# A decoder trunk in one core: the first feed-forward group in ordinary form, the squares summed on VectorE

## The reference, cut to what matters

```
def rmsnorm(x, g):
    y = x * lax.rsqrt(jnp.mean(x * x, axis=-1, keepdims=True) + EPS)
    return y * g

def swiglu(x, w_in, w_out):
    gate, up = jnp.split(x @ w_in, 2, axis=-1)
    return (jax.nn.silu(gate) * up) @ w_out

for layer in range(DEPTH):
    mix = recurrent_mixer(...) if layer < N_A else forgetting_attention(...)
    h = h + mix
    h = h + swiglu(rmsnorm(h, norm_ffn[layer]), w_ffn_in[layer], w_ffn_out[layer])
return rmsnorm(h, norm_final)
```

## Time and profile before

| | us |
|---|---|
| median of 3 runs | 2400.66 (2400.25 to 2406.35) |
| the profiled execution | 2403.73 |
| its span, first to last instruction | 2401.9 |
| TensorE busy in it | 2329.1 |
| VectorE busy in it | 1423.8 |
| ScalarE busy in it | 893.8 |
| GpSimd busy in it | 164.9 |

### The profile page before, as it was taken

How to read it: one execution, slowest core, us unless ns; L and a number is a source line. 1 busy time by engine, 2 the same in 40 slices (tenths; PEclk the granted TensorE clock), 3 DMA queues, 4 the chain that set the end, 5 groups by cost and what they waited for, 6 DMA issues and landing times.

```text
span 2401.9 us, 28970 instructions
## 1 busy us (share of the span) xinstructions
PE 2329.1 (97%) x10945; PEld 1922.3 (80%) x10945; DVE 1423.8 (59%) x1589; ACT 893.8 (37%) x1289; POOL 164.9 (7%) x97
## 2 busy tenths in 40 slices
PE   8999968999999999989999999999999999999998
PEld 7788846888888888778888878778888888888886
DVE  7667787666666666676666656753433334344435
ACT  5553644222222222255656656643211111111114
POOL 3000020000000000041111111102000000000000
PEclk9999989999999999999999999999999999999999
DMA  4121101111111111121111011122111111111111
GB/s 141 44 61 52 53 0 50 54 53 54 53 53 52 52 53 53 54 80 32 31 36 35 27 36 36 53 89 70 53 45 51 44 52 44 52 44 52 44 44 70
DMA packets 167310, 123.41 MB, mean 51 GB/s; under 512 B 5081, under 2 KB 148673, under 8 KB 167233
## 3 DMA queue, kind: packets, MB, share of 16 engines
q1 hardware_dynamic: 165504, 118.04, 16.1%
q10 hardware_dynamic: 1728, 4.31, 0.7%
HBM read 113.89 MB, written 8.45 MB: 51 GB/s over the span
## 4 chain that ended last, share of the span: by engine, by line
PE 79%; DVE 2%; issue 1%; ACT 1%; DMA 0%; POOL 0%; ACTq 0%; DVEq 0%; SPq 0%
PE ps L879 39%; PE ps L1051 16%; PE ps L1231 10%; PE ps L1278 3%; PE ps L1265 3%; PE ps L1365 3%; PE ps L1246 2%; PE ps L1243 1%; PE ps L1204 1%; PE ps L1344 1%; PE ps L1245 0%; PE ps L1311 0%; DVE xl L1960 0%; PE ps L1190 0%; DVE resid L1976 0%
## 5 line engine op out<-in xcount | busy, mean ns | idle before, releaser
L1976 DVE TENSOR_TENSOR resid<-ps,resid 128x1024 f32<-128x1024 f32 x204 | 247.9, 1221 | 151.8 <-PE ps L879 151.8
L1970 DVE TENSOR_TENSOR tmp<-ps,rstd 128x1024 f32<-128x1024 f32 x52 | 63.4, 1223 | 268.9 <-PE ps L879 268.4
L879 PE MATMUL ps<-x1h,wh_att 128*128 128x512 f32 x528 | 163.1, 390 | 0.0
L879 PE MATMUL ps<-x1l,wh_att 128*128 128x512 f32 x528 | 162.6, 389 | 0.0
L879 PE MATMUL ps<-x1h,wl_att 128*128 128x512 f32 x528 | 162.6, 389 | 0.0
L2212 DVE TENSOR_TENSOR ring_l<-raw_ffn,ring_h 128x512 fp32r<-128x512 f32 x154 | 108.2, 709 | 90.4 <-ACT ring_h L1588 90.2
L1588 ACT ACTIVATE ring_h<-raw_ffn 128x512 fp32r<-128x512 f32 x154 | 95.2, 626 | 177.1 <-PE ps L879 99.7
L1231 PE MATMUL ps<-xh,wh_att 128*128 128x512 f32 x368 | 150.1, 408 | 1.4 <-issue 1.4
L1231 PE MATMUL ps<-xl,wh_att 128*128 128x512 f32 x368 | 144.8, 393 | 2.4 <-issue 2.4
L1231 PE MATMUL ps<-xh,wl_att 128*128 128x512 f32 x368 | 144.9, 394 | 0.0
L1939 DVE TENSOR_TENSOR wl_att<-raw_att,wh_att 128x1024 fp32r<-128x1024 f32 x75 | 104.2, 1390 | 60.8 <-ACT wh_att L1409 60.8
(11 more groups left out here) (354 smaller groups left out, 5539.7 us busy)
## 6 DMA issues: line engine op xcount, KB each, us to landing
raw_ffn<-in_w_ffn_in SPq DMA_DIRECT2D x44, 512.0 KB, 5.0
raw_att<-in_w_ffn_in SPq DMA_DIRECT2D x33, 512.0 KB, 3.8
raw_ffn<-in_w_ffn_out SPq DMA_DIRECT2D x22, 512.0 KB, 4.3
raw<-in_w_rec_in SPq DMA_DIRECT2D x16, 512.0 KB, 5.6
raw_att<-in_w_kvf SPq DMA_DIRECT2D x16, 512.0 KB, 4.0
raw<-in_w_ffn_in SPq DMA_DIRECT2D x11, 512.0 KB, 3.8
raw<-in_w_ffn_out SPq DMA_DIRECT2D x11, 512.0 KB, 3.5
raw_att<-in_w_ffn_out SPq DMA_DIRECT2D x11, 512.0 KB, 3.5
```

The costliest lines, as they stand in the source:

```text
L879: last = pe.matmul(acc[:, h], w, v[:, h], start=(first and p == 0), stop=(final and p == 2))
L1976: dve.tensor_tensor(resid[:, m, :], ps[slot][:, :], resid[:, m, :], ALU.add).then_inc(drained[slot], 1)
```

## The change

The first group no longer uses seven products on sums, but eight on plain quarters for each pair: 16 products. B12 is made for it, in the buffers of T4 (high) and T3 (low), which it leaves after the thirteenth product. The four weight blocks of pair 0 are each one unit and serve two products (both token halves), those of pair 1 as well. Gate and up of the two pairs stand in four PSUM tiles of their own; there are no taps and joins in this group, and VectorE scales each tile at once (`first_gate`, `first_up`). The sums T1 and T2 are made behind the plain quarters, T3 and T4 behind the norm, between steps of the first group's end. ScalarE scales the difference twice now (into the high half of T1 and into `t2_sum`), where VectorE scaled it once before. The sums of squares of this place go from GpSimd to VectorE (`sum_square`). The stat stands behind the tenth product. The first load of group 1 waits for four units instead of thirteen. In group 1, pair 0 waits for two scaled tiles, and its P5 unit is made before the group. Functions take an object F with the block's semaphores and buffers; what they do is else the same. Of the diff, lines that only rename are left out:

```diff
+class FeedForward:
+    def __init__(self, f, seg, order, first_units):
+        self.f, self.seg, self.order = f, seg, order
+        self.first_units = first_units + ["g1", "g2", "u1", "u2"]
+        self.first_products = [(0, n, half) for half in range(2) for n in range(4)]
+        self.first_products += [(1, n, half) for of in (4, 6) for half in (1, 0) for n in (of, of + 1)]
+    def first_part(self, n, half):
+        return {"1": ("B11", "B12"), "2": ("B21", "B22")}[self.first_units[n][1]][half]
...
     GROUP_UNITS, OUT_UNIT, SECOND_UNIT = 18, 7, 11
-    UNITS_FIRST = len(FIRST_GROUP)
-    PART_HIGHS = [(c, k) for k in range(4) for c in ("B21", "B22")]
...
+    UNITS_FIRST, PRODUCTS_FIRST, B12_USED, STAT_AFTER = 8, 16, 13, 9
+    T_SUMS = [("D", 0), ("D", 1), ("T2", 0), ("D", 2), ("T2", 1), ("D", 3), ("T2", 2), ("T2", 3)]
+    T_SUMS += [(c, k) for c in ("T3", "T4") for k in range(4)]
...
+    PART_HIGHS = [(c, k) for c in ("B21", "B11", "B22", "B12") for k in range(4)] + T_HIGHS
+    PART_LOWS = [(c, k) for c in ("B21", "B11", "B22", "B12") for k in range(4)] + T_LOWS
...
+            part_h["B12"], part_l["B12"] = part_h["T4"], part_l["T3"]
...
-                return (product_filled, off - RING + 1) if off >= RING else (in_filled, 4 * BLOCKS)
+                return (F.product_filled, off + 1) if off >= RING else (in_filled, 4 * BLOCKS)
...
-                sp.wait_ge(unit_lo, UNITS_FIRST - 1 if first else unit(g, SECOND_UNIT - GROUP_UNITS)[1] - 1)
...
+                sp.wait_ge(F.unit_lo, 4 if first else unit(g, SECOND_UNIT - GROUP_UNITS)[1] - 1)
+                load_pair(F, g, 0, load_of(g, 0))
...
             pool.wait_ge(hi_ready[slot], n)
-            run_squares("recE")
             gain_piece(pieces.use("forget", 0), V_KV, HEADS)
...
+            def first_group(F):
+                begun = set()
+                for n, (j, u, half) in enumerate(F.first_products):
+                    up = F.first_units[u][0] == "u"
+                    tile = first_tile(F, j, up)
+                    if tile not in begun:
+                        claim(tile)
+                    start = (tile, half) not in begun
+                    begun.update((tile, (tile, half)))
+                    product(F, bank(tile[0], half), unit(0, u), F.first_part(u, half), start, True, PART_LOWS)
+                    if n == STAT_AFTER:
+                        run_stat(F.seg)
...
+                lows = PART_LOWS if isinstance(g, int) and g == 1 and j == 0 else None
+                if lows is not None:
+                    for t in range(2):
+                        slot, n = first_tile(F, 0, t)
+                        pe.wait_ge(drained[slot], n)
+                else:
...
-            last_y_high(1)
...
+                elif c == "T1":
+                    g = V_FFN + F.f * KT + k
+                    act.wait_ge(F.t_summed, T_SUMS.index(("D", k)) + 1)
+                    act.activation(F.part_h[c][:, k, :], F.t_sum[k % 2][:, :], ACT.Copy,
+                                   scale=vec[:, g:g + 1]).then_inc(F.part_hi, 1)
+                    act.activation(F.t2_sum[:, k, :], F.t_sum[k % 2][:, :], ACT.Copy,
...
+            def rec_to_ffn(F):
+                for n in range(4):
+                    first_high(F, n)
+                last_y_high(1)
                 for k in range(4):
+                    part_high(F, "B21", k)
                     square("recE", k)
+                for c in ("B11", "B22", "B12"):
+                    for k in range(4):
+                        part_high(F, c, k)
+                square("recE", 4)
+                first_high(F, 4)
+                square("recE", 5)
+                part_high(F, "T1", 0)
+                first_high(F, 5)
+                square("recE", 6)
+                part_high(F, "T1", 1)
+                first_high(F, 6)
+                square("recE", 7)
+                part_high(F, "T2", 0)
+                first_high(F, 7)
+                part_high(F, "T1", 2)
+                part_high(F, "T2", 1)
+                part_high(F, "T1", 3)
+                part_high(F, "T2", 2)
+                part_high(F, "T2", 3)
+                root("recE")
+                pair_silu(F, 0, 0)
+                pair_high(F, 1, 0, P1)
+                pair_high(F, 1, 0, P2)
                 for k in range(4):
+                    part_high(F, "T3", k)
+                hidden_high(F, 0, 0)
+                pair_high(F, 1, 0, P6)
+                pair_high(F, 1, 0, P5)
                 for k in range(4):
...
+                pair_silu(F, prev, 1)
+                if not (isinstance(g, int) and g == 1):
+                    pair_high(F, g, 0, P5)
+                tap(F, g, 0, "s1")
...
+                    dve.wait_ge(F.t_scaled, k + 1)
+                    ins = dve.scalar_tensor_tensor(out=t2, in0=r22, scalar=g2, in1=t2, op0=ALU.mult, op1=ALU.subtract)
...
+            def sum_square(seg, k):
+                dve.wait_ge(sq_ready, STAT[seg] * KT + k + 1)
+                if k > 1:
+                    dve.wait_ge(sq_summed, SUMMED[seg] + k - 1)
+                dve.tensor_tensor(sq(seg, 0), sq(seg, 0), sq(seg, k), ALU.add).then_inc(sq_summed, 1)
+            def rec_to_ffn(F):
                 def add(n):
                     add_tile(tiles.use("recE", n), feature("recE", n), 8 * (BLOCKS - 1) + n + 1)
+                first_low(F, 0)
+                first_low(F, 1)
+                add(0)
+                for n in range(1, 5):
+                    add(n)
+                    part_low(F, "B21", n - 1)
+                first_low(F, 2)
+                for n in range(5, 8):
+                    add(n)
+                    part_low(F, "B11", n - 5)
+                part_low(F, "B11", 3)
+                first_low(F, 3)
+                for c in ("B22", "B12"):
+                    for k in range(4):
+                        part_low(F, c, k)
+                for k in range(1, 4):
+                    sum_square("recE", k)
+                part_sum(F, "D", 0)
+                first_low(F, 4)
+                sum_square("recE", 4)
+                part_sum(F, "D", 1)
+                first_low(F, 5)
+                sum_square("recE", 5)
+                part_sum(F, "T2", 0)
+                part_low(F, "T1", 0)
+                first_low(F, 6)
+                sum_square("recE", 6)
+                part_sum(F, "D", 2)
+                part_low(F, "T2", 0)
+                first_low(F, 7)
+                sum_square("recE", 7)
+                part_sum(F, "T2", 1)
+                part_low(F, "T1", 1)
+                part_sum(F, "D", 3)
+                part_low(F, "T2", 1)
+                part_sum(F, "T2", 2)
+                part_low(F, "T1", 2)
+                part_low(F, "T2", 2)
+                part_sum(F, "T2", 3)
+                part_low(F, "T1", 3)
+                part_low(F, "T2", 3)
                 norm_ready("recE")
+                first_gate(F, 0)
+                first_up(F, 0)
+                weight_sum(F, 1, 0, 1, 2)
+                pair_low(F, 1, 0, P1)
+                gate_times_up(F, 0, 0)
+                pair_low(F, 1, 0, P2)
+                late_parts(F, "T3")
+                hidden_low(F, 0, 0)
+                weight_sum(F, 1, 0, 3)
+                pair_low(F, 1, 0, P6)
+                pair_low(F, 1, 0, P5)
+                first_gate(F, 1)
```

More of the change, by code:

```diff
@@ L544, in bank, with first_filled, banks @@
+        def first_filled(F, j, up):
+            last = max(n for n, (_, u, _) in enumerate(F.first_products)
+                       if u // 4 == j and (F.first_units[u][0] == "u") == bool(up))
+            return F.product_filled, last + 1
         def bank(tile, half):
             return ps[tile][:, half * BANK:(half + 1) * BANK]
-        def banks(j, first=False):
-            return bank(0, j), bank(1, 0), bank(1, 0) if first and j == 1 else bank(1, 1)
+        def banks(j):
+            return bank(0, j), bank(1, 0), bank(1, 1)
@@ L551, in ffn_free, with resid_tile @@
+        def resid_tile(F, m):
+            return tiles.use(F.seg, F.order.index(m))
         def ffn_free(f, j, g):
@@ L1640, in first_group, with tap @@
-            def first_group():
-                def high(n):
-                    pair_high(0, *FIRST_GROUP[n])
-                high(0)
-                high(1)
+                unit_high(F, unit(g, off), raw_block(F, b, n), (F.loaded[b], count), unit_freed(F, g, off))
+            def tap(F, g, j, what):
+                w, _, y = banks(j)
+                act.wait_ge(F.product_filled, product_at(g, PRODUCTS * j + {"s1": P1, "u2": P6, "s5": P5}[what]))
+                act.wait_ge(hl_ready if what == "s5" else h_ready, times(g, 2, 2 * F.f * GROUPS + j - 1))
+                gate, up = F.gate_up[j]
+                dst = {"s1": gate[:, 0:BANK], "u2": gate[:, BANK:S], "s5": up[:, BANK:S]}[what]
+                act.activation(dst, y if what == "s5" else w, ACT.Copy).then_inc(F.tapped, 1)
@@ new lines, in groups @@
+            def groups(F):
```

(12 more changed lines are left out.)

722 lines of the change are left out of this document (313 added, 409 removed).

## The result

The changed kernel takes 2378.34 us in the median of four runs (2376.64 to 2380.36), the kernel before 2403.06 in the four runs beside it (2400.25 to 2406.35): a ratio of 0.9897, with a 95% interval from 0.9879 to 0.9915. It is faster by 24.7 us. The profiled execution took 2376.64 us, of which the span is 2374.8, 27.1 us less than the span of the profile before.

A forecast was written before the change was run, and what follows sets the result against it. TensorE, busy 97%, was the bound, with VectorE bounding it from 338 to 364 us. P6 of group 1 at 391.1 with low clock, against 411.31, gave 20.2 us off 2400.66: 2380.5 us, range 2374 to 2388.5.

The forecast's parts named there:

- Residual tiles: Before the first group: tile 4 starts at 319.9 us instead of 323.97, its 4.57 us wait becoming about 0.5.
- The sixteen products: First group on TensorE: two products more, +5.5 us, no waits inside; the stat ends at 359.9, all sixteen at 376.3.
- the ledger: Account up to P6 of group 1: gone 26.0 us of waits and some 9.5 of low clock, added together 15.4.
- Squares on VectorE: Seven sums of squares moved from GpSimd to VectorE: between 1.7 us gained and 8.3 lost, booked at 8.3 in VectorE's chain.
- The rival that blamed ScalarE: VectorE's slow operations come from ScalarE's work and stay, 2.1 us each on the path; up to 2419 us; chance 0.04.
- The chain to the tap: VectorE and ScalarE up to group 1's first tap: root from 361.9 to 366.6 us, T4 until 388.0, tap done 389.5.
- The new wait: P6 of group 1 waits for ScalarE's tap until 389.5 us: 7.8 us instead of 6.03, bounds nothing and 14.
- The clock behind it: Low TensorE clock after P6's wait for the tap, priced at 1.6 us from one row.
- Behind P6: From P6 of group 1 both kernels issue the same instructions; from 430 us all starts earlier and runs as before.
- the second wait: Rival: VectorE falls behind from 340 to 366 us, the root is late, cover 1.1 us; 2385 to 2389 us; chance 0.14.
- The shorter wait: Rival: P6's wait for the tap is shorter, at most 7.8 + 1.6 us; down to 2371 us; chance 0.08.
- the time did not return in group 1: Rival: the waits' time returns elsewhere in group 1, nothing gained; 2394 to 2405 us; chance 0.04.

## Why the prediction came out as it did

I had forecast 2380.5 us (2374.0 to 2388.5); it is 2378.34. The sum for the first group held almost to the step. That the time is off by only 2.2 us is in part luck: the gain was forecast as 20.2 us and is 24.7, because a term of about 5 us behind the group was missing; but the kernel before took 2403.06 us in the runs beside this one and not the 2400.66 from which the forecast was counted, which hides half of the error.

*Residual tiles.* Tile 4 starts at 319.90, forecast 319.9; its wait is 0.39, forecast 0.5. Full clock from 324 to 330 us, as forecast.

*The sixteen products.* No wait in any of them, the stat at 358.12 (forecast 358.2). The choice to call these 5.5 us "on the path, certain" was wrong as a price, though: the run with fewer matmuls shows them free. The forecast did not suffer, because I had P6 wait for the tap and not for TensorE; only the ledger did. The ledger booked 5.5 us of products beside 7.8 of wait, when the two are one sum: 13.3 us between TensorE's work and the tap, however it is divided.

*Squares on VectorE.* Differences at 0.69 us, GpSimd idle. That GpSimd was the cause is shown twice, by taking its sums away (0.69) and by putting them back (2.90). The rival that blamed ScalarE has fallen: with the sums moved, ScalarE's copy (0.72 us) and the difference (0.69) both start at 336.10, and in the kernel before ScalarE's squares end just before the long differences begin (338.42 and 338.58 us). The rule of the Trainium skill, SBUF — State Buffer, "Who interferes with whom", that the two engines block one another agrees with the trace in both directions: VectorE's sum for T2 rose from 0.75 to 2.90 us, and GpSimd's sum, where it was the one held up, from 2.36 to 3.60 us. The advice in the Trainium skill, Perfetto Trace Analysis, "Optimizing Scalar/DVE Operations", to move work off a saturated VectorE would by itself have had the change lose, though the same place warns that it may not help between these two engines; moving seven sums onto it cost nothing that can be measured in the old order (0.9991, 0.9973 to 1.0010) and gave 1.6 us at P6 in the new one. Of the two ends that I had set (1.7 us of gain, 8.3 of loss) it came out at the gain. Most of the forecast hung on the order, and rightly.

*The chain to the tap.* The root's first load at 362.10 (forecast 361.9), its end at 366.79 (366.6), the last high half of T4 at 388.12 (388.0), Silu and tap until 389.55 (389.5). ScalarE's timeline:

```profile
387.49 0.63 ACT L1695 ACTIVATE t4h<-t_sum 128x512 fp32r<-128x512 f32 x1 [0.83 <-DVE t_sum L2383]
388.02 1.04 ACT L1666 ACTIVATE gate<-gate 128x1024 f32<-128x1024 f32 x1
388.97 0.58 ACT L1658 ACTIVATE gate<-ps 128x512 f32<-128x512 f32 x1
```

The new wait is 7.79 us (7.8). Every instruction of the chain was costed from a row, and its order read from the diff; the chain holds to 0.2 us over 70 us. With the clock of 0.72 at the first residual tiles it comes 1.7 us later; that this differs between executions I had not allowed for, and the range covered it.

*The clock behind it.* Priced at 1.6 us from the wait of 6.03, it was 2.1 for this wait of 7.79: this term was mis-sized by 0.5 us, and the group gives 19.6 us instead of 20.2. The length of the wait doesn't explain it. In the kernels in the old order the same twelve matmuls cost 1.5 us of low clock behind 5.83 us of wait, 1.6 behind 6.03, 2.2 behind 5.94, 2.4 behind 5.89 and 2.6 behind 5.62. One row of one profile could not give this price to better than about 1 us.

*Behind P6.* Here a step failed: that from 430 us on "everything behind it starts earlier, and runs as it did". It does so until about 1390 us; then the kernel before loses time to waits that the one after doesn't have. 5.8 us in the two profiles, for one pair of waits of 3.7 us together, and 1.4 near 1605 us; in the medians 24.7 - 19.6 = 5.1 us for all that lies behind P5. The row was there to be seen: two waits without a releaser in a loop whose matmuls have all operands. I had looked for TensorE's idle time only in the stretch of the change. It couldn't have been foreseen that the change would take them away; that the 2403 us held such a part could have been a rival with its price: the 3.7 us of these waits, and the low clock behind them.

The rivals: the second wait did not come (no wait for the stat's bank), though the profile with the sums on GpSimd shows how near it was: 0.6 us. The shorter wait did not come, and the time did not return in group 1.

## What to carry to other kernels

Where one engine's queue orders the work, write out its instructions with a duration from a row for each, and do so up to the instruction that the bottleneck waits for: here the sum held to 0.2 us over 70, and the chain showed where a better order was to be had (the T4 round behind the taps, another 6.9 us). The clock behind a wait is known less well: take several rows for it. Work added to the bottleneck ahead of a wait for another engine costs nothing but makes that wait shorter; book the two as one term. Before two versions of a kernel with loops are compared, look for waits without a releaser in both traces, outside the changed stretch too, and try a few idle instructions ahead of the loop: what they move there is not the merit of either version. Compare marks only between profiles whose clock agrees ahead of them.

## What was not expected of the hardware

TensorE stopped 2 or 4 times in an execution for 1.3 to 2.8 us in the attention loop, with its operands there, in all six profiles with the old number of its matmuls ahead of the loop, and in none of seven with 24 or more added. It costs more than the waits, as the clock falls behind them: 5.8 us for waits of 3.7 us in the kernel before, 7.6 for 4.9 us in the kernel with fewer matmuls, whose windows read

```profile
1243.00:1259.00 16.00, 11.06 (x43) 8.11 (x43) 7.30 (x8) 8.71 (x10) 4.26 (x2) 0.79 0.14 37
1259.00:1275.00 16.00, 16.00 (x96) 13.61 (x94) 8.60 (x13) 6.48 (x14) 0.00 (x0) 1.00 0.12 33
```

a clock of 0.79 and 4.94 us idle, where the next window has 1.00 and none. In the medians the 24 matmuls were worth 8.2 us to the kernel before, 2 of them ahead of the loop, and 14.8 to the one with fewer matmuls.

The same wait of 2.4 us at 313 us left the clock at 1.00 in some executions and at 0.72 over the next 6 us in others, for the kernel after 1.7 us of its time. Two profiles of one kernel can differ by that alone. And behind waits of 5.6 to 6.0 us for `up` twelve matmuls that take 2.73 us at full clock took 4.21 to 5.28.
